# Two token groups in one static plan, silu through tanh, and keys, values and bias reloaded per head, in a Conformer-style encoder layer

## What is computed

```python
xp = _half_ffn(xp, g_ffn1[l], w1_gate[l], w1_up[l], w1_down[l])
q_p, kv_p = proj(_rmsnorm(xp, g_mix[l]))
o_p = _query_blocks(lambda qb, pb: mix(*qb, pb, *kv_p, pos_p), q_p, pos_p)
xp = xp + o_p @ w_out[l]
xp = _half_ffn(xp, g_ffn2[l], w2_gate[l], w2_up[l], w2_down[l])

def _half_ffn(x, g, w_gate, w_up, w_down):
    h = _rmsnorm(x, g)
    return x + 0.5 * ((jax.nn.silu(h @ w_gate) * (h @ w_up)) @ w_down)
```

## Time and profile before

| | |
|---|---|
| median of the runs | 2938.88 us |
| span of the profiled execution | 2931.6 us |
| TensorE busy | 2587.1 us, 88% |
| weight loads busy | 2321.7 us, 79% |
| VectorE busy | 1221.5 us, 42% |
| ScalarE busy | 802.8 us, 27% |
| GpSimd busy | 120.8 us, 4% |
| mean granted clock of TensorE | 0.921 |
| DMA | 162.4 MB, 17.3% of 16 engines' span |

### The profile page before, as it was taken

The page is one execution under the profiler, slowest core; times in us unless marked ns, Lnnn a source line. Parts: engine busy times, 40 slices in busy tenths (PEclk is TensorE's granted clock), DMA queues, the critical chain, the costliest instruction groups (busy, mean ns, idle before and its releaser), DMA issues. The chain is left out here.

```text
span 2931.6 us, 35181 instructions
## 1 busy us (share of the span) xinstructions
PE 2587.1 (88%) x13474; PEld 2321.7 (79%) x13474; DVE 1221.5 (42%) x2471; ACT 802.8 (27%) x1430; POOL 120.8 (4%) x174
## 2 busy tenths in 40 slices
PE   5999999999996999536757878969699999999999
PEld 3999999999995888424656766658599999999998
DVE  5333333333325322478887544331433333333332
ACT  3111111111113110489853541130311111111110
POOL 1000000000002312000110000000100000000000
PEclk8999999999997999757776889979799999999999
DMA  5111111111002221411111024230211111111101
GB/s 182 41 43 43 43 43 43 43 43 43 14 0 105 76 75 48 131 47 29 44 37 37 26 79 149 78 129 0 94 43 43 43 43 43 43 43 41 36 9 64
DMA packets 133665, 162.40 MB, mean 55 GB/s; under 512 B 27312, under 2 KB 98256, under 8 KB 133584
## 3 DMA queue, kind: packets, MB, share of 16 engines
q1 hardware_dynamic: 133584, 161.40, 17.3%
HBM read 127.85 MB, written 23.30 MB: 52 GB/s over the span
## 5 line engine op out<-in xcount | busy, mean ns | idle before, releaser
L515 PE MATMUL b_bank<-XTh_b,f_gu_hi 128*128 128x384 f32 x1056 | 353.9, 335 | 3.0 <-DVEq L496 3.0
L515 PE MATMUL a_bank<-XTh_a,f_gu_hi 128*128 128x384 f32 x1056 | 353.7, 335 | 3.0 <-DVEq L496 3.0
L517 PE MATMUL b_bank<-XTh_b,f_gu_lo 128*128 128x384 f32 x1056 | 353.6, 335 | 0.0
L516 PE MATMUL b_bank<-XTl_b,f_gu_hi 128*128 128x384 f32 x1056 | 353.5, 335 | 0.0
L516 PE MATMUL a_bank<-XTl_a,f_gu_hi 128*128 128x384 f32 x1056 | 353.4, 335 | 0.0
L517 PE MATMUL a_bank<-XTh_a,f_gu_lo 128*128 128x384 f32 x1056 | 353.4, 335 | 0.0
L480 DVE TENSOR_TENSOR f_hid<-f_silu,b_bank 128x384 f32<-128x384 f32 x66 | 36.6, 554 | 420.7 <-ACT f_silu L452 420.7
L480 DVE TENSOR_TENSOR f_hid<-f_silu,a_bank 128x384 f32<-128x384 f32 x66 | 36.6, 554 | 420.4 <-ACT f_silu L452 420.4
L515 PEld LDWEIGHTS b_bank<-XTh_b,f_gu_hi 128*128 128x128 f32 x1056 | 198.9, 188 | 3.8 <-DVEq L496 3.4
L515 PEld LDWEIGHTS a_bank<-XTh_a,f_gu_hi 128*128 128x128 f32 x1056 | 198.7, 188 | 3.8 <-DVEq L496 3.4
L516 PEld LDWEIGHTS b_bank<-XTl_b,f_gu_hi 128*128 128x128 f32 x1056 | 198.9, 188 | 0.4
(11 more groups left out here) (262 smaller groups left out, 4741.1 us busy)
## 6 DMA issues: line engine op xcount, KB each, us to landing
f_gu_raw<-in_w_gate SPq DMA_DIRECT2D x22, 1024.0 KB, 5.5
f_gu_raw<-in_w_up SPq DMA_DIRECT2D x22, 1024.0 KB, 8.0
f_d_raw<-in_w_down SPq DMA_DIRECT2D x22, 1024.0 KB, 4.9
win_w_raw<-in_w_in SPq DMA_DIRECT2D x4, 2048.0 KB, 8.5
s_k_in<-in_cache_diff_k SPq DMA_DIRECT2D x8, 1024.0 KB, 5.4
s_v_in<-in_cache_diff_v SPq DMA_DIRECT2D x8, 1024.0 KB, 5.3
q_scr<-win_rows SPq DMA_DIRECT2D x18, 256.0 KB, 2.0
wout_w_raw<-o_scr SPq DMA_DIRECT2D x9, 512.0 KB, 4.2
```

The source lines that it names most:

```text
L515: pe.matmul(out, hi, XTh[:, k, tok], start=(k == 0), stop=False)
L516: pe.matmul(out, hi, XTl[:, k, tok], start=False, stop=False)
L517: last = pe.matmul(out, lo, XTh[:, k, tok], start=False, stop=(k == KD - 1))
```

## The change

All stages become one block. The program makes a list of items (`make_plan`), and each engine walks the whole list and emits its part of each item, so one order holds on all five queues; nothing is in a hardware loop.

- Tokens form group A (tiles 0 to 3 and the samples, 640 tokens, two chunks of 320) and group B (tiles 4 to 7, one chunk of 512). FFN pairs are walked for A and then for B; every weight is loaded and split for each of them. Weights pass through a ring of four split units of 1024 elements and two raw slots.
- `merge` puts a list of side items between main items, in proportion to weights written in the plan. Tables and B's first norm lie in A's first FFN; the samples' and A's attention in pairs 2 to 10 of B's first FFN; B's attention in pairs 0 to 9 of A's second FFN; other norms in projections. The last 11 pairs (B's second FFN) have nothing between them.
- The down products of a pair are spread over the next pair's gate items.
- PSUM: two banks for gate and up, two for down, four in turn for all side items; the projections use banks from 0 on.
- silu(x) y is made as (tanh(x/2) + 1) x y with the factor 0.25 at the addition to X.
- Attention is by head with tiles inside, in blocks of one differential head or two sparse heads. Key rows (three in a ring), values (two) and bias windows (three) are loaded from DRAM per head; transposed keys go to `kT_scr`, windows to `near_scr`. Queries are loaded per block, in both halves at once, and transposed twice as often. X of a group is spilled to `x_scr` and reloaded around its attention.
- Each group has its own threshold search: tile 3 on VectorE and 2 on ScalarE for A, 4 and 5 on VectorE and 6 and 7 on ScalarE for B. The maxima take windows of 512 instead of 256 columns. Output rows are scaled by their norm on VectorE instead of GpSimd.
- Three fences: SP waits for stores, then releases ScalarE, VectorE and GpSimd.

```diff
+GA, GB = 0, 1
+TILES = ((0, 1, 2, 3, NP), (4, 5, 6, 7))
+WIDTH = tuple(len(t) * P for t in TILES)
+CHUNKS = (((0, 320), (320, 640)), ((0, 512),))
+K_PART = (4, 2)
...
+    def pair(self, p):
+        g = PAIRS[p][1]
+        for w in range(2):
+            for j in range(F_PAIR):
+                parts = [(c, k) for c in range(len(CHUNKS[g])) for k in range(0, KD, K_PART[g])]
+                downs = [] if w or self.prev is None else [("down", self.prev, j, i) for i in range(len(TILES[PAIRS[self.prev][1]]))]
+                sent = 0
+                for n, (c, k) in enumerate(parts):
+                    self.put(("gu", p, w, j, c, k))
+                    if w and k + K_PART[g] == KD:
+                        self.late = ("late", p, j, c)
+                    upto = round(len(downs) * (n / (len(parts) - 1) if j == 0 else (n + 1) / len(parts)))
+                    while sent < upto:
+                        self.put(downs[sent])
+                        sent += 1
+        self.prev = p
...
+def merge(main, side, first=0, share=0.97):
+    total = sum(main_time(m) for m in main[first:])
+    weight = sum(w for w, _ in side)
+    out, spent, n, cum = list(main[:first]), 0.0, 0, 0.0
+    for m in main[first:]:
+        out.append(m)
+        spent += main_time(m)
+        while n < len(side) and cum * total * share <= spent * weight:
+            out.append(side[n][1])
+            cum += side[n][0]
+            n += 1
+    out += [s for _, s in side[n:]]
+    return out
...
+    for i in range(n + 2):
+        b = first + i
+        att1 = i >= 1 and i - 1 < n and BLOCKS[b - 1][0] != "idx"
+        att2 = i >= 2 and BLOCKS[b - 2][0] != "idx"
+        if i < n:
+            scores(b, 0)
+        if att2:
+            out.append((0.4, ("o_take", b - 2)))
+        searching(i, 0)
+        if att1:
+            L = (BLOCKS[b - 1][2] + 1) * P
+            for a in range(1 if BLOCKS[b - 1][0] == "diff" else 2):
+                out.append((0.3 + 0.9 * L / 1000, ("probs", b - 1, a)))
+                if a == 0 and i < n:
+                    scores(b, 1)
+        if i < n and not att1:
+            scores(b, 1)
+        if att2 and BLOCKS[b - 2][0] == "diff":
+            out.append((0.3, ("o_square", b - 2)))
+        searching(i, 1)
+        if i + 1 < n:
+            out.append((0.8, ("q_turn", b + 1)))
+            if i + 2 < n:
+                out.append((0.1, ("q_load", b + 2)))
...
+    for f in range(2, N_PAIR):
+        s.pair(pair_no(0, GB, f))
+    s.flush()
+    plan += merge(s.take(), [(0.1, ("enter", GA))] + sample_items() + [(0.1, ("fence",))] + att_items(GA) + [(0.1, ("reload", GA))]
+                  + out_items("ota", 5), share=0.98)
...
+    for f in range(N_PAIR - 1):
+        s.pair(pair_no(1, GA, f))
+    plan += merge(s.take(), [(0.1, ("enter", GB))] + att_items(GB) + [(0.1, ("reload", GB))] + out_items("otb", 4), share=0.98)
...
+                    part = act_in[:, j, lo:up]
+                    if w == 0:
+                        if p:
+                            act.wait_ge(hid_ready, plan.late_no["late", p - 1, F_PAIR - 1, len(CHUNKS[PAIRS[p - 1][1]]) - 1] + 1)
+                        done(act, key)
+                        act.activation(part, out_of(key)[:, 0:up - lo], ACT.Tanh, scale=0.5).then_inc(tanh_ready, 1)
+                    else:
+                        if p:
+                            done(act, ("down", p - 1, F_PAIR - 1, len(TILES[PAIRS[p - 1][1]]) - 1))
+                        emptied(act, key)
+                        act.activation(hid_hi[:, j, lo:up], part, ACT.Copy).then_inc(hid_hi_ready, 1)
...
+                    if w == 0:
+                        dve.wait_ge(tanh_ready, plan.tanh_no[key] + 1)
+                        dve.scalar_tensor_tensor(part, part, 1.0, out_of(key)[:, 0:up - lo], ALU.add, ALU.mult).then_inc(frees(key), 1)
+                    else:
+                        emptied(dve, ("gu", p, 0, j, c))
+                        done(dve, key)
+                        dve.tensor_tensor(part, part, out_of(key)[:, 0:up - lo], ALU.mult).then_inc(frees(key), 1)
...
-                        act.activation(silu[:, n % 2], psum[2 * (n % 2)][:, 0:TOK_CHUNK], ACT.Silu).then_inc(silu_ready, 1)
...
```

More of the change, by code:

```diff
@@ new lines, with group_of, pair_no, att_blocks @@
+SEARCH_DVE = ((3,), (4, 5))
+SEARCH_ACT = ((2,), (6, 7))
+TOP_BIT = -(1 << 31)
+HALF = SAMPLE_KEYS // 2
+ROUNDS = -(-SAMPLE_TOPK // 8)
+KT = PAST // P
+BATCH_PAIRS = DEC_BATCH // 2
+TAGS = ("n1a", "n1b", "n2a", "n2b", "n3a", "n3b")
+def group_of(tag):
+    return GA if tag.endswith("a") else GB
+def pair_no(ffn, g, f):
+    return (ffn * 2 + g) * N_PAIR + f
+def att_blocks(g):
+    tiles = [t for t in TILES[g] if t < NP]
+    searched = [t for t in tiles if (t + 1) * P > TOPK]
+    out = [("idx", n, t, g) for t in searched for n in range(2)]
+    out += [("diff", h, t, g) for h in range(DIFF_HEADS) for t in tiles]
+    out += [("dsa", hp, t, g) for hp in range(DSA_HEADS // 2) for t in tiles]
+    return out
@@ new lines, in unit_of, with load_of, main_time @@
+def unit_of(item):
+    if item[0] == "gu":
+        return ("gu", item[1], item[2], item[3])
+    if item[0] == "down":
+        return ("d", item[1], item[2])
+    return item[1:5]
+def load_of(unit):
+    return (unit[0:3], unit[3]) if unit[0] == "gu" else (unit[0:2], unit[2]) if unit[0] == "d" else (unit[0:3] + (unit[3] // 2,), unit[3] % 2)
+def main_time(item):
+    if item[0] == "gu":
+        return 1.77 if PAIRS[item[1]][1] == GA else 1.37
+    return 1.37 if item[0] in ("down", "mm") else 0.0
@@ new lines, in build @@
+        rows_in, rows_seen = {}, [0, 0]
+        for where, n in plan.rows_no.items():
+            if where[0].startswith("ot"):
+                rows_seen[n % 2] += 16
+                rows_in[where] = rows_seen[n % 2]
+        keys_in, values_in, near_in = {}, {}, {}
+        for m in range(20):
+            keys_in[m] = 16 * sum(x % K_RING == m % K_RING for x in range(m + 1))
+        for m in range(10):
+            values_in[m] = 16 * (m // 2 + 1)
+        for m in range(2 * HEADS):
+            near_in[m] = 16 * (m // NEAR_RING + 1)
@@ new lines, in turn, with tab_spread @@
+                def turn(tag, i, half):
+                    key = ("turn", tag, i, half)
+                    g = group_of(tag)
+                    part = (slice(None), slice(4 * half, 4 * half + 4), xt_tile(g, i))
+                    dve.wait_ge(xt_hi_ready, plan.turn_no[key] + 1)
+                    dve.tensor_tensor(XTl[g][part], out_of(key)[:].rearrange("p (k n) -> p k n", k=4), XTh[g][part].bitcast(F32),
+                                      ALU.subtract).then_inc(frees(key), 1)
+                def tab_spread():
+                    dve.wait_ge(tables_in, 32)
+                    for h in range(HEADS):
+                        last = dve.tensor_scalar(table_b[:, h, :], ones[:], table[:, h:h + 1], 1.0 / QK_SCALE, ALU.mult, ALU.mult)
+                    last.then_inc(spread_ready, 1)
@@ new lines, in x_key @@
+                def x_key(kind, p):
+                    tile = idx_T if kind == "i" else dsa_T
+                    key = ("x_key", kind, p, 1)
+                    if p >= 2:
+                        for n in range(2):
+                            done(dve, ("x_index", p - 2, n) if kind == "i" else ("x_score", DEC_BATCH + 2 * p - 3, n))
+                    done(dve, key)
+                    dve.tensor_copy(tile[:, p % 2, PAST:SAMPLE_KEYS], out_of(key)[:, 0:DEC_SEQ]).then_inc(frees(key), 1)
@@ L1698, in _ @@
+                for item in plan.items:
+                    if item[0] in stages:
+                        stages[item[0]](*item[1:])
             @block.gpsimd
```

3646 lines of the change are left out of this document (1952 added, 1694 removed).

## The result

The changed kernel takes 2894.34 us (median of 4 runs, 2883.94 to 2897.2), the kernel before beside it 2937.03 (2933.42 to 2941.34). The ratio is 0.9848, interval 0.9828 to 0.9867: 1.5% less time, where 8.5% was forecast and 3.4% was the least that the range allowed. About 205 us of the forecast gain are missing. The profiled execution has a span of 2895.3 us.

The account below looks back on a forecast made before the run. TensorE's own work at full clock was taken as the bound: 1974 + 447 + 30 + 33 = 2484 us, plus 114 for late VectorE, 45 for new chains and 45 for short waits, 2688, forecast as 2690; range 2570 to 2840.

Parts of the forecast that it names:

- Pace: TensorE's matmul steps: 0.1467 us each for the new 320 columns, 0.2267 us for 512 columns.
- rival C: The weight load sets the pace of TensorE's 320-column steps, 0.1733 us each: 112 us more, 2800; chance 0.05.
- Parts 1 and 2: TensorE's work: remaining FFN and projection matmuls 1974 us, moved-in attention, norm and table matmuls 447, switches 30.
- Part 3: Ends of the kernel: 32 us before the first FFN matmul, less 4 already counted, and 5 at the end: 33 us.
- Part 4: Attention with the threshold search: VectorE, at 0.873 busy, later than TensorE by 65 and 49 us, 114; bounds 50 and 198.
- Part 5: TensorE waits at DRAM round trips of keys, at query row loads and three fences: 45 us, bounds 20 and 90.
- Part 6: Short TensorE waits and clock elsewhere: 4% of the 1126 mixed us, 45 us; bounds 0 and 150.
- A: Queues never get in the way; VectorE costs only 50 us, other waits their low bounds: 2570 us; chance 0.15.
- B: TensorE's clock falls to 0.8 in the mixed 1126 us: about 110 us more, 2800; chance 0.15.
- D: SP, blocked in the common order, asks for weights late: 90 us more, 2780; chance 0.10.
- E: Slower than before: each of 640 side items costs TensorE a 0.68 us wait, 435 us, total 2971; chance 0.05.
- The value 0: ScalarE needs no table loads between tanh and exp: 0 us, against up to 149 us if it did.

Follow-up runs that it names:

- Narrow counts: Changed kernel with the threshold search's counting steps looking at 8 columns instead of 384 to 1024: 2848.15 us.
- one item moved: Changed kernel with VectorE taking a finished attention output out of PSUM right behind the next block's mixing, before its next score evictions: 2863.63 us.
- a late step moved: Changed kernel with hid_lo placed ahead of a weight split that falls due between a gate-up chunk and it: 2871.53 us.
- the pauses: Changed kernel with three empty weighted items in the side lists, so that main matmuls fall at the DRAM round trips: 2899.03 us.
- the four edits: Changed kernel with hid_lo ahead of the split, attention output taken early, the split's subtraction on GpSimd, and empty items at round trips: 2780.47 us.
- narrow splits: Changed kernel with ScalarE's copy and VectorE's subtraction of weight splits touching 2 columns of each block from the fifth weight unit on: 2737.83 us.
- another queue: Changed kernel with all loads and stores of the sample and prompt attention issued by GpSimd instead of SyncE: 2889.82 us.
- three edits: Changed kernel with hid_lo ahead of the split, attention output taken early, and the split's subtraction on GpSimd: 2815.48 us.

## Why the prediction was wrong, step by step

**Pace.** Right. In the timeline of the changed kernel 12 steps of 320 columns go from 201.13 to 202.89, 0.1467 us each, as estimated, so rival C is out. Steps of 512 columns were a little slower than the earlier trace rows:

```profile
2701.31 0.39 PE L1137 MATMUL bank<-XTl_b,w_hi 128*128 128x512 f32 x1
...
2704.09 0.39 PE L1137 MATMUL bank<-XTl_b,w_hi 128*128 128x512 f32 x1
```

12 steps in 2.78 us, 0.2317 against 0.2267.

**Parts 1 and 2, work.** Right in sum: main matmuls 1994 us for 1974 (the slower steps), side items 437 for 477.

**Part 3, ends.** First 320-column matmul at 26 us for 32; start and end 41 us beyond the work for 33.

**Part 4, VectorE late where the search runs.** Its size nearly held, 142 us beyond the work for 114, in part by luck: up to 39 of the 142 come with the lower clock, for which the part had nothing. Narrow counts gave back 46. And its reason was drawn too narrowly. I let VectorE be late only where its busy time at 0.873 exceeded TensorE's, and declared TensorE last again everywhere else. VectorE in the search of B is busy for 0.81 (I had asked for over 0.85), and TensorE waits as readily where VectorE is at half load (110.81 of 195 us in the sparse heads).

**Part 5, new chains.** 95 us beyond the work at the round trips for 45, and over the 90 of my upper bound. The 14.1 us at L1280, where the sample attention waits for its query rows, are one more such wait and stand in that stretch's 56. The output rows on their way back (L1193, 27.2 us) had no term in my sum. The round trip before the first score of A is the gap that I priced at 8 to 10 us; from the start of VectorE's copy to the query transposes it takes 13.1, and TensorE waits 11.5 of them (the longest at L1218 above). The pieces of the chain that ended last:

```profile
1039.23 0.70 DVE k_out_a L1856
...
1039.98 4.18 DMA kT_scr<-k_out_a
...
1048.08 0.43 SPq L2412
...
1048.56 3.77 DMA q_rows_a<-q_scr
...
1052.38 0.69 PE bank L1218 x2
```

From the landing of the store on SyncE issues nine transfers, 0.47 us each, the last of them the query rows: I counted the queue's transfers, not its issues.

**Part 6, the step that failed.** Short waits and clock elsewhere, put at 4% of the 1126 mixed us, 45 us. Measured: 56 in the sample attention, 99 in the attentions without a search, 19 in FFN 2 and 12 more, 186 in all, four times as much and over the upper bound of 150. Of the 186, 14 are the wait of part 5 just named, and at most some 35 come with the lower clock. Of the 227 us that were missing beyond the work, 8 are the ends, 28 part 4, 50 part 5 and 141 this step. The 4% was worked out from no row; behind it stood part 4, which took a ratio of busy times as a sign that the queues don't matter. What the runs show in its place is the time that stands ahead in a queue: all engines run one order, and an item's eviction stands behind whatever the plan put before it on ScalarE and VectorE. That is why one bank less costs 56 us, one item moved gives 31, a late step moved gives 23, and why taking over a quarter of ScalarE's work gives 65 although it is idle for two thirds of the time. Of the splits I counted VectorE's extra 158 us within part 4 and found ScalarE's hidden; together they cost 156 us of time. The changed kernel makes them once for each group, twice as many as before, so about half of that, some 80 us, comes with the change; this share is an estimate, no run has loaded the weights once. Nor do the gains of single edits add up to the 141 us; they overlap, and three of them with the pauses, at unchanged values, return 114 us of the 205 that were missing.

**The rivals.** A fell. B: the clock is 0.88 to 0.95 in the mixed windows shown and 0.82 to 0.86 at the three longer round trips, not 0.8 throughout. It was higher in most of the kernels that had fewer waits (0.952 in the changed kernel, 0.969 with the four edits, 0.971 with narrow splits, but about 0.953 with the late step moved), which leaves open what drives what. Its cost, at most 89 us, is no small part of the miss, so this rival was wrong in its clock and less so in its price of 110. D: none of the longest waits is ended by a weight load, and another queue changed nothing that can be measured. E came nearest, though it had 0.05: its 2971 is 77 us off, the 2800 of B and C 94, and the kernel did not get slower. From 700 to 2390 us 394 us lie beyond the work, over some 640 side items 0.62 us an item, where the earlier trace rows gave 0.68 and the rival decided from 0.65. That closeness is partly luck, since up to 86 of the 394 come with the lower clock and some 109 are round trips; what is left is 0.33 to 0.45 us an item. I had set aside because main matmuls now stand on both sides of an item. They do, but they bring their own evictions and splits, which stand in the same queues.

**No table loads.** ScalarE loads one table in the whole changed kernel, 1.3 us. The value 0 was right. The Trainium skill, page "ScalarE: Activation LUTs", section "Table sets: the hidden batching unit", lists tanh in the set that is loaded for exp, and the trace agrees.

**Open.** Why the attention of two groups in blocks takes 662 us and that of all tokens 512 was not taken apart: two searches, smaller rings, single banks and the lower clock (some 470 us of the 662, 266 of the 512) are all in it.

## What to carry to other kernels

Before work of a second kind is put between matmuls, price each of its items with the wait that one costs where it stands alone, and drop that price only if the items it brings to the evicting engines are not in one order with those of the main work. A busy share of one third on an engine says nothing of what it holds up; add up the time of the items that the plan puts between a result and its use, on every engine, and move evictions and late steps ahead of weight preparation. Main work put under a known round trip pays only if the place that it is taken from wasn't using it: here it gave nothing by itself and 35 us after three edits that took waits away.

## What the hardware showed

GpSimd subtracts 128x1024 elements in 2.43 us, VectorE in 1.22, and 320 of them on GpSimd left the steps of VectorE that read PSUM as they were (554 to 555 ns at the first gate step), but hid_lo, from SBUF to SBUF, rose from 552 to 687 ns. And 512-column steps that follow each other in FFN 2 of B take 0.2317 us for 0.2267 before, with the clock granted in full, while the down products of the first FFN of the same kernel keep 0.226 ((200.91 - 199.78)/5); the cause is open.
